# Two causal attentions with scores one head further ahead on the tensor engine, and four buffers that hold first scores, then probabilities

## The chip, the cores and the metric

The kernel runs on one core of a Trainium2 chip. The core has a tensor engine (PE in the profile, with its weight loads as PEld), a vector engine (DVE), a scalar engine (ACT), a general engine (POOL) and a queue that issues transfers (SP). Each engine runs its own list of instructions in order; they meet only at semaphores. The metric is the device time of one execution in microseconds, the median of three runs.

## The reference

The model has four blocks over 256 tokens of width 1024: an RWKV-7 time mix, a causal attention with 16 heads of width 64, an mLSTM with an MLP, and a latent attention (8 heads, values of width 128, keys of 128 plus 64 rotary) with another MLP. The two attentions compute the same thing per head:

```python
s = (jnp.einsum('bqhd,bkhd->bhqk', qn_b, k_nope)
     + jnp.einsum('bqhd,bkd->bhqk', qr_b, k_rope)).astype(jnp.float32) * scale
s = jnp.where(kpos[None, :] <= qpos[:, None], s, -jnp.inf)
p = jax.nn.softmax(s, axis=-1)
return jnp.einsum('bhqk,bkhd->bqhd', p.astype(v.dtype), v)
```

For the first attention the rotary term is inside `q` and `k`, and with 256 tokens its single block of 256 keys is the whole sequence. The scores of a head are thus a 256 x 256 lower triangle: 128 queries against 128 keys, and 128 queries against 256 keys, 384 columns in all.

## The kernel before

The whole program is one launch. Weights come from memory in 95 panels of 2 MB through a ring of four slots (`ring`); SP issues panel i once slot i - 4 has been used (L1221). Large products run as three products of rounded parts, so each panel is first split by ACT (high part, L1279 and L1292) and by DVE (low part, L1850 and L1863).

The function `attention` stands three times, once for each engine. It is called as "at1" (16 heads, L961) and as "at3" (8 heads, L1203). For each head h:

- PE, `score(h)`: the scores into one PSUM bank, "S". In at1 these are lines L958 and L959, in at3 L1197 to L1200.
- DVE: adds the causal mask, writes the masked scores to the buffer `Ss[h % 2]` in SBUF and takes the row maxima (L2239, twice, each with an accumulator read), then turns the maxima into biases (L2243).
- ACT: two exponentials from `Ss[h % 2]` into `Ps[h % 2]` with row sums (L1547, L1549).
- PE, `turn_p(h)`: three transposes of the probabilities into a bank "PT" (L614).
- ACT: copies them to `PTs[h % 2]` (the copy helper, L1336).
- PE, `pv(h)`: three products with the values into a bank "O" (L623, L625).
- DVE, `gather`: after every fourth head (at1) or second head (at3) the division by the row sums (L2226, L2229), and in at1 the gating (L2266).

The order on PE is written out: in step h it issues the scores of head h, the transposes of head h - 1, and the value products of head h - 2. Banks for S and PT come in turn from five banks. ACT's order is: exponentials of head h, copy of head h - 1, and in some steps a quarter of a weight panel's split (L1292: one quarter in each of the steps 1 to 8 of at1, two in each of the steps 1 to 4 of at3). DVE's order is: maxima of head h, a gather where one is due, in at3 a quarter of a row of the modulation table in odd steps (L1837), and quarters of the low parts (L1850: one in each of the steps 6 to 13 of at1, two in each of the steps 4 to 7 of at3).

Both buffers are two deep. DVE may write `Ss[h % 2]` once the exponentials of head h - 2 are done (L2236), and ACT may write `Ps[h % 2]` once the transposes of head h - 2 are done (L1545).

Of the kernel before, what the change touches and what calls it, by code (L numbers as in the profile page):

```python
# [10 lines left out]
ACT = mybir.ActivationFunctionType  # L11
# [90 lines left out]
def build(nc, x, cc_d, pc_d, pos_d, gn_d, sel_d, cond_d, stream, out, debug=None):  # L102

    order = []
    with ExitStack() as ctx:
# [5 lines left out]
        def sem(name):  # L111
            if name not in sems:
                sems[name] = ctx.enter_context(nc.semaphore(name))
            return sems[name]
# [60 lines left out]
        def finished(product):  # L175

            b, turn = place[product]
            return sem(f"bank_full{b}"), turn + 1
# [78 lines left out]
        def cols(n, a, b):  # L257
            return arena[:, n, a:b]

        Ss = cols(12, 0, 768).rearrange("p (a n) -> p a n", a=2)  # L260
        Ps = cols(12, 768, 1536).rearrange("p (a n) -> p a n", a=2)
        PTs = cols(14, 0, 768).rearrange("p (a n) -> p a n", a=2)


# [87 lines left out]
        def _(pe):  # L352
# [249 lines left out]
            def attention(name, heads, dv, scores, V):  # L602

                per = 512 // (TB * dv)

                def score(h):
                    b = claim((name, "S", h))
                    scores(h, b).then_inc(filled((name, "S", h)), 1)

                def turn_p(h):  # L610
                    b = claim((name, "PT", h))
                    pe.wait_ge(sem(name + "_p"), h + 1)
                    for n in range(3):
                        ins = nc.tensor.transpose(b[:, n * P:(n + 1) * P], Ps[:, h % 2, n * P:(n + 1) * P], ident)  # L614
                    ins.then_inc(filled((name, "PT", h)), 1)

                def pv(h):
                    if h % per == 0:
                        claim((name, "O", h // per), 5 + h // per % 2)
                    b = bank((name, "O", h // per))  # L620
                    pe.wait_ge(*evacuated((name, "PT", h)))
                    o = (h % per) * TB * dv
                    mm(b[:, o:o + dv], PTs[:, h % 2, 0:P], V[:, 0, h * dv:(h + 1) * dv], start=True, stop=True)  # L623
                    for kb in range(2):
                        ins = mm(b[:, o + dv:o + 2 * dv], PTs[:, h % 2, (1 + kb) * P:(2 + kb) * P],  # L625
                                 V[:, kb, h * dv:(h + 1) * dv], start=(kb == 0), stop=(kb == 1))
                    if h % per == per - 1:
                        ins.then_inc(filled((name, "O", h // per)), 1)
                    else:
                        ins.then_inc(pn.step(name + "_pv"), 1)  # L630


                kept, rotation["banks"] = rotation["banks"], list(range(5))
                for h in range(heads + 2):
                    if h < heads:
                        score(h)
                    if 1 <= h <= heads:
                        turn_p(h - 1)
                    if h >= 2:
                        pv(h - 2)  # L640
                rotation["banks"] = kept


# [616 lines left out]
        def _(act_):  # L1260
# [279 lines left out]
            def attention(name, heads, dv, scale, early):  # L1540
                for h in range(heads + 1):
                    if h < heads:

                        if h >= 2:
                            act_.wait_ge(*finished((name, "PT", h - 2)))  # L1545
                        act_.wait_ge(sem(name + "_max"), h + 1)
                        act(Ps[:, h % 2, 0:P], Ss[:, h % 2, 0:P], ACT.Exp, scale=scale, bias=nmax[:, h, 0:1],  # L1547
                                   accum_out=rs[:, h, 0:1]).then_inc(ac.step(), 1)
                        act(Ps[:, h % 2, P:3 * P], Ss[:, h % 2, P:3 * P], ACT.Exp, scale=scale, bias=nmax[:, h, 1:2],  # L1549
                                   accum_out=rs[:, h, 1:2]).then_inc(ac.step(name + "_p"), 1)  # L1550
                    if h >= 1:

                        if h >= 3:
                            act_.wait_ge(*pv_done(name, 512 // (TB * dv), h - 3))
                        copy(PTs[:, (h - 1) % 2, :], (name, "PT", h - 1), 3 * P)
                    for u, q in early.get(h, ()):
                        split_quarter(u, q)
# [200 lines left out]
        def _(dve):  # L1758
# [460 lines left out]
            def attention(name, heads, dvd, scale, O, early, between=None, gathered=None):  # L2219
                per = 512 // (TB * dvd)  # L2220

                def gather(g):
                    p = (name, "O", g)
                    dve.wait_ge(*finished(p))
                    hs = slice(g * per, (g + 1) * per)
                    V.reciprocal(rs[:, hs, :], rs[:, hs, :]).then_inc(dv.step(), 1)  # L2226
                    dve.wait_ge(*dv.last)
                    o = O[:, :, g * per * dvd:(g + 1) * per * dvd].rearrange("p b (h d) -> p h b d", d=dvd)
                    tt(o, bank(p)[:, :].rearrange("p (h b d) -> p h b d", h=per, b=TB),  # L2229
                                  rs[:, hs, :].unsqueeze(3).to_broadcast([P, per, TB, dvd]), ALU.mult).then_inc(dv.frees(p), 1)  # L2230

                done = 0
                for h in range(heads):

                    if h >= 2:
                        dve.wait_ge(sem(name + "_p"), h - 1)  # L2236
                    dve.wait_ge(*finished((name, "S", h)))
                    for tb, cs in ((0, slice(0, P)), (1, slice(P, 3 * P))):
                        V.tensor_tensor_reduce(Ss[:, h % 2, cs], bank((name, "S", h))[:, cs], con("causal")[:, cs], 1.0, 3.0 * NEG,  # L2239
                                               ALU.add, ALU.max, accum_out=mx[:, 2 * (h % 2) + tb:2 * (h % 2) + tb + 1]).then_inc(  # L2240
                            dv.frees((name, "S", h)) if tb else dv.step(), 1)
                    dve.wait_ge(*dv.last)
                    ts(nmax[:, h, :], mx[:, 2 * (h % 2):2 * (h % 2) + 2], -scale, None, ALU.mult).then_inc(dv.step(name + "_max"), 1)  # L2243
                    if (done + 1) * per <= h - 3:
                        gather(done)
                        done += 1
                    if between:
                        between(h)
                    for u, q in early.get(h, ()):
                        split_quarter(u, q)  # L2250
                while done * per < heads:
                    if gathered:
                        gathered(done)
                    gather(done)
                    done += 1
                if gathered:
                    gathered(done)
# [349 lines left out]
```

## Time and profile before

| | us |
|---|---|
| three runs | 1100.61, 1101.17, 1101.26 (median 1101.17) |
| the profiled execution | 1103.99 |
| its span, first to last instruction | 1102.2 |
| PE busy in the span | 1027.2 (93%) |
| DVE, ACT busy | 720.3 (65%), 511.0 (46%) |
| mean granted clock of PE | 0.977 of full speed |
| at1 runs from about | 387 to 422 |
| at3 runs from about | 851 to 874 |

A timeline row gives start, duration, engine, line, output and inputs, and in brackets how long the engine had been idle before it and what released it. Busy time of PE has modelled ends: rows that follow each other closely overlap. So the pace of PE is read from start to start, not from durations. A row "x3" merges three instructions in a row of the same line.

### The profile page before, as it was taken

To read this page: it belongs to the slowest core of one execution; us is meant where nothing else is said; L and a number is where in the kernel's file an instruction comes from. 1 tells how busy PE (TensorE), PEld (TensorE's weight loads), DVE (VectorE), ACT (ScalarE), POOL (GpSimd) and SP (SyncE) were. 2 spreads that over 40 slices of the span, in tenths; PEclk is the share of its full clock that TensorE was granted. 3 is DMA by queue.
4 is the path that set the end of the run, shared out by engine and by line. 5 is a ranking of instruction groups with operands and counts; after the bars stand their busy time and mean duration, and the time that the engine had idled before them with its cause. 6 is when DMAs were issued, how large, how long until landed. Compare 5 with 4: busy or idle time off the path is not lost.

```text
span 1102.2 us, 19472 instructions
## 1 busy us (share of the span) xinstructions
PE 1027.2 (93%) x8386; PEld 873.2 (79%) x8386; DVE 720.3 (65%) x1210; ACT 511.0 (46%) x780; POOL 33.2 (3%) x31
## 2 busy tenths in 40 slices
PE   5999999889998989999988999999889889999997
PEld 5784679887787867777766989998688759899995
DVE  6778248738889657655485785766588856644544
ACT  3424132135633585444354544555455746544542
POOL 0000025200000100000000000000000000000000
PEclk9999999999999999999988999999889999999998
DMA  9763301512476531556245577767725652665420
GB/s 382 301 247 126 153 1 32 224 61 78 153 303 231 187 119 51 190 219 229 77 153 229 199 288 297 285 238 303 298 78 208 250 197 110 215 243 208 175 78 38
DMA packets 15221, 205.39 MB, mean 186 GB/s; under 512 B 1816, under 2 KB 1816, under 8 KB 2976
## 3 DMA queue, kind: packets, MB, share of 16 engines
q1 hardware_dynamic: 14544, 202.55, 48.1%
q8 instruction: 66, 1.08, 0.4%
q10 hardware_dynamic: 592, 1.61, 0.4%
q14 instruction: 19, 0.16, 0.0%
HBM read 203.10 MB, written 1.05 MB: 185 GB/s over the span
## 4 chain that ended last, share of the span: by engine, by line
PE 78%; DVE 12%; DMA 4%; ACT 3%; issue 3%; SPq 0%; DVEq 0%; ACTq 0%
PE bank L452 16%; PE bank L453 16%; PE bank L454 16%; PE bank L746 5%; PE bank L545 5%; PE bank L401 4%; DMA ring<-in_stream 4%; DVE slot_parts L1863 2%; PE bank L558 2%; DVE ring L1837 2%; PE bank L652 1%; PE bank L730 1%; ACT page_parts L1279 1%; DVE arena L2324 1%; DVE arena L2239 1%
## 5 line engine op out<-in xcount | busy, mean ns | idle before, releaser
L452 PE MATMUL bank<-page_parts 128*128 128x512 f32 (+2 forms) x1190 | 406.5, 342 | 11.3 <-DVE slot_parts L1863 4.1
L1863 DVE TENSOR_TENSOR slot_parts<-ring,page_parts 128x2048 fp32r<-128x2048 f32 (+2 forms) x113 | 253.5, 2251 | 129.4 <-ACT page_parts L1279 128.8
L1279 ACT ACTIVATE page_parts<-ring 128x2048 fp32r<-128x2048 f32 (+2 forms) x113 | 211.5, 1883 | 138.1 <-PE bank L454 74.7
L452 PEld LDWEIGHTS bank<-page_parts 128*128 128x128 f32 x1190 | 228.1, 192 | 36.1 <-issue 10.6
L453 PE MATMUL bank<-slot_parts,page_parts 128*128 128x512 f32 (+2 forms) x622 | 243.5, 391 | 0.0
L454 PE MATMUL bank<-page_parts 128*128 128x512 f32 (+2 forms) x622 | 243.2, 391 | 0.0
L454 PE MATMUL bank<-page_parts,slot_parts 128*128 128x256 f32 x568 | 160.8, 283 | 0.0
L453 PE MATMUL bank<-page_parts 128*128 128x256 f32 x568 | 160.8, 283 | 0.0
L1336 ACT ACTIVATE arena<-bank 128x512 f32<-128x512 f32 (+2 forms) x134 | 73.8, 574 | 171.9 <-PE bank L454 57.4
L454 PEld LDWEIGHTS bank<-page_parts 128*128 128x128 f32 x622 | 118.9, 191 | 23.9
L453 PEld LDWEIGHTS bank<-slot_parts,page_parts 128*128 128x128 f32 x622 | 119.0, 191 | 22.5
L453 PEld LDWEIGHTS bank<-page_parts 128*128 128x128 f32 x568 | 109.0, 192 | 0.5
L454 PEld LDWEIGHTS bank<-page_parts,slot_parts 128*128 128x128 f32 x568 | 109.0, 192 | 0.0
L1837 DVE CUSTOM_DVE_ANT_0 ring<-ring,small 128x1024 f32<-128x1024 f32 x88 | 103.7, 1219 | 3.1 <-DMA ring<-in_stream 3.1
L558 PE MATMUL bank<-cc,arena 128*128 128x128 f32 x174 | 29.9, 340 | 33.8 <-DVE arena L1806 28.0
L746 PE MATMUL bank<-arena 64*64 64x64 f32 x1792 | 53.9, 218 | 6.4 <-issue 6.3
L746 PEld LDWEIGHTS bank<-arena 64*64 64x64 f32 x1792 | 53.1, 135 | 7.0 <-issue 7.0
L558 PEld LDWEIGHTS bank<-cc,arena 128*128 128x128 f32 x174 | 26.5, 179 | 39.4 <-DVE arena L1806 19.9
L545 PE MATMUL bank<-ring,arena 128*128 128x512 f32 x128 | 57.2, 607 | 0.0
L1614 ACT ACTIVATE arena<-bank 128x512 f32<-128x512 f32 x32 | 19.1, 596 | 69.9 <-PE bank L454 62.7
L545 PEld LDWEIGHTS bank<-ring,arena 128*128 128x128 f32 x128 | 24.8, 195 | 30.3 <-issue 30.3
L2078 DVE TENSOR_TENSOR arena<-arena,bank 128x512 f32<-128x512 f32 x36 | 23.9, 683 | 33.0 <-PE bank L746 32.7
(298 smaller groups left out, 1190.8 us busy)
## 6 DMA issues: line engine op xcount, KB each, us to landing
ring<-in_stream SPq DMA_DIRECT2D x95, 2048.0 KB, 8.3
arena<-in_x SPq DMA_DIRECT2D x2, 512.0 KB, 4.3
gn<-in_gn ACTq DMA_DIRECT2D x2, 512.0 KB, 17.3
out<-arena SPq DMA_DIRECT2D x2, 512.0 KB, 2.6
cc<-in_consts SPq DMA_DIRECT2D x1, 899.0 KB, 6.4
small<-in_cond ACTq DMA_DIRECT2D x1, 512.0 KB, 10.4
pc<-in_params SPq DMA_DIRECT2D x1, 287.5 KB, 6.7
gn<-in_head_sel ACTq DMA_DIRECT2D x1, 32.0 KB
```

What stands on the lines that cost most here:

```text
L401: ins = mm(b[:, half * T:(half + 1) * T], weights[:, k, ct * P:(ct + 1) * P], src[:, k, :], start=(k == 0), stop=(k == k_tiles - 1))
L452: mm(out, a[0], b[0], start=start, stop=False)
L453: mm(out, a[0], b[1], start=False, stop=False)
L454: return mm(out, a[1], b[0], start=False, stop=stop)
L545: ins = mm(b[:, 0:n], src[:, k, tb * P:(tb + 1) * P], weights[:, k, 0:n], start=(k == 0), stop=(k == k_tiles - 1))
L558: ins = nc.tensor.transpose(b[:, jj * T + tb * P:jj * T + (tb + 1) * P], src[:, tb, j * P:(j + 1) * P], ident)
L746: ins = mm(b[q * LC:(q + 1) * LC, j * LC:(j + 1) * LC], lhs(q, j), rhs(q, j), start=True, stop=True)
L1279: act(unit_parts(n)[0], unit_values(n)[1], ACT.Copy).then_inc(ac.step("w_hi"), 1)
L1336: act(dst, bank(product)[:, 0:n].rearrange("p (a b) -> p a b", a=dst.shape[1]) if len(dst.shape) == 3 else bank(product)[:, 0:n], kw.get(" ...
L1837: V.tensor_tensor_reduce(W, W, cond_row, 1.0, 0.0, ALU.mult, ALU.add, accum_out=ADA[:, at:at + 1]).then_inc(dv.step("ada_done" if ct == 3 ...
L1863: tt(unit_parts(n)[1], lo, hi, ALU.subtract).then_inc(dv.step("w_lo"), 1)
L2078: tt(dst[:, g], dst[:, g], bank((name, l, g))[:, :].rearrange("p (j t) -> p j t", j=8), ALU.subtract).then_inc(dv.frees((name, l, g)), 1)
```

## The change

The score and probability buffers become one array `Ps` of four buffers at the place of the former two and two. DVE writes the masked scores of head h to `Ps[h % 4]`, ACT takes the exponentials in place, and PE transposes from there. The wait of DVE before it writes becomes: the transposes of head h - 4 are done. The wait of ACT for the transposes of head h - 2 goes. On PE, step h now issues the scores of head h, the transposes of head h - 2 and the value products of head h - 3, in heads + 3 steps. `PTs` stays two deep, and everything else stays as it was.

```diff
-        Ss = cols(12, 0, 768).rearrange("p (a n) -> p a n", a=2)
-        Ps = cols(12, 768, 1536).rearrange("p (a n) -> p a n", a=2)
+        Ps = cols(12, 0, 1536).rearrange("p (a n) -> p a n", a=4)
...
-                        ins = nc.tensor.transpose(b[:, n * P:(n + 1) * P], Ps[:, h % 2, n * P:(n + 1) * P], ident)
+                        ins = nc.tensor.transpose(b[:, n * P:(n + 1) * P], Ps[:, h % 4, n * P:(n + 1) * P], ident)
...
-                for h in range(heads + 2):
+                for h in range(heads + 3):
                     if h < heads:
                         score(h)
-                    if 1 <= h <= heads:
-                        turn_p(h - 1)
-                    if h >= 2:
-                        pv(h - 2)
+                    if 2 <= h < heads + 2:
+                        turn_p(h - 2)
+                    if h >= 3:
+                        pv(h - 3)
...
-                        if h >= 2:
-                            act_.wait_ge(*finished((name, "PT", h - 2)))
                         act_.wait_ge(sem(name + "_max"), h + 1)
-                        act(Ps[:, h % 2, 0:P], Ss[:, h % 2, 0:P], ACT.Exp, scale=scale, bias=nmax[:, h, 0:1],
+                        act(Ps[:, h % 4, 0:P], Ps[:, h % 4, 0:P], ACT.Exp, scale=scale, bias=nmax[:, h, 0:1],
                                    accum_out=rs[:, h, 0:1]).then_inc(ac.step(), 1)
-                        act(Ps[:, h % 2, P:3 * P], Ss[:, h % 2, P:3 * P], ACT.Exp, scale=scale, bias=nmax[:, h, 1:2],
+                        act(Ps[:, h % 4, P:3 * P], Ps[:, h % 4, P:3 * P], ACT.Exp, scale=scale, bias=nmax[:, h, 1:2],
                                    accum_out=rs[:, h, 1:2]).then_inc(ac.step(name + "_p"), 1)
...
-                    if h >= 2:
-                        dve.wait_ge(sem(name + "_p"), h - 1)
+                    if h >= 4:
+                        dve.wait_ge(*finished((name, "PT", h - 4)))
                     dve.wait_ge(*finished((name, "S", h)))
                     for tb, cs in ((0, slice(0, P)), (1, slice(P, 3 * P))):
-                        V.tensor_tensor_reduce(Ss[:, h % 2, cs], bank((name, "S", h))[:, cs], con("causal")[:, cs], 1.0, 3.0 * NEG,
+                        V.tensor_tensor_reduce(Ps[:, h % 4, cs], bank((name, "S", h))[:, cs], con("causal")[:, cs], 1.0, 3.0 * NEG,
```

On PE at the start of at1, before the change (L958 and L959 are scores, L614 transposes, L623 and L625 value products; `at1_p` counts heads whose exponentials are done, `bank_free` a bank that has been read out):

```order
L958 MATMUL bank0<-arena 128x128 [waits bank_free0,zeros,bank_free5]
L959 MATMUL bank0<-arena 128x256
L958 MATMUL bank1<-arena 128x128 [waits bank_free1]
L959 MATMUL bank1<-arena 128x256
L614 MATMUL bank2<-cc,arena 128x128 [waits at1_p,bank_free2]
L614 MATMUL bank2<-cc,arena 128x128 x2
L958 MATMUL bank3<-arena 128x128 [waits bank_free3]
L959 MATMUL bank3<-arena 128x256
L614 MATMUL bank4<-cc,arena 128x128 [waits at1_p,bank_free4]
L614 MATMUL bank4<-cc,arena 128x128 x2
L623 MATMUL bank5<-arena 128x64 [waits bank_free2,bank_free5]
L625 MATMUL bank5<-arena 128x64 x2
```

And in the changed kernel at the same place (all its lines from there on have numbers lower by one):

```order
L957 MATMUL bank0<-arena 128x128 [waits bank_free0,zeros,bank_free5]
L958 MATMUL bank0<-arena 128x256
L957 MATMUL bank1<-arena 128x128 [waits bank_free1]
L958 MATMUL bank1<-arena 128x256
L957 MATMUL bank2<-arena 128x128 [waits bank_free2]
L958 MATMUL bank2<-arena 128x256
L613 MATMUL bank3<-cc,arena 128x128 [waits at1_p,bank_free3]
L613 MATMUL bank3<-cc,arena 128x128 x2
L957 MATMUL bank4<-arena 128x128 [waits bank_free4]
L958 MATMUL bank4<-arena 128x256
L613 MATMUL bank0<-cc,arena 128x128 [waits at1_p,bank_free0]
L613 MATMUL bank0<-cc,arena 128x128 x2
```

Three groups of scores now stand ahead of the first transposes instead of two, and so it stays through both attentions.

On DVE, the masked maxima of heads 3 and 4 of at1 before (the row with two waits is a head's first; the bias row has the wait for DVE's own last step):

```order
L2239 ISA arena,small<-bank0,cc 128x128 [waits bank_full0,at1_p]
L2239 ISA small 128x1
L2239 ISA arena,small<-bank0,cc 128x256
L2239 ISA small 128x1
L2243 TENSOR_SCALAR small<-small 128x2 [waits bank_free0]
L2239 ISA arena,small<-bank2,cc 128x128 [waits bank_full2,at1_p]
```

And the same heads in the changed kernel:

```order
L2235 ISA arena,small<-bank4,cc 128x128 [waits bank_full4]
L2235 ISA small 128x1
L2235 ISA arena,small<-bank4,cc 128x256
L2235 ISA small 128x1
L2239 TENSOR_SCALAR small<-small 128x2 [waits bank_free4]
L2235 ISA arena,small<-bank1,cc 128x128 [waits bank_full1,bank_full3]
```

The wait for the exponentials (`at1_p`) has gone; from head 4 on a wait for a bank of transposes (`bank_full3`) stands in its place.

## Rows read from the trace of the kernel before

**Rows 1.** The page: the span
```profile
span 1102.2 us, 19472 instructions
```

**Rows 2.** Busy time by stretch, then clock, DMA share and GB/s
```profile
387.00:420.00 33.00, 27.71 (x194) 22.31 (x193) 20.45 (x95) 26.81 (x89) 0.00 (x0) 1.00 0.22 84
400.00:410.00 10.00, 8.90 (x63) 7.05 (x63) 7.73 (x33) 8.26 (x28) 0.00 (x0) 1.00 0.00 1
560.00:570.00 10.00, 8.36 (x32) 7.72 (x33) 8.79 (x13) 3.99 (x10) 0.00 (x0) 0.53 0.39 167
851.00:872.00 21.00, 17.49 (x121) 15.04 (x120) 17.15 (x61) 15.04 (x48) 0.00 (x0) 1.00 0.68 287
```

**Rows 3.** Waits in at1, 386 to 426 us: total, times, longest
```profile
ACT arena L1547 <- DVE small L2243: 6.2, 10, 0.9
PE bank L614 <- ACT arena L1549: 5.3, 9, 1.8
```

**Rows 4.** Timeline of at1, its start: start, duration, engine, line
```profile
390.24 0.39 PE L958 MATMUL bank<-arena 128*128 128x128 f32 x2
390.52 0.47 ACT L1336 ACTIVATE arena<-bank 128x384 f32<-128x384 f32 x1
390.89 0.62 ACT L1292 ACTIVATE page_parts<-ring 128x512 fp32r<-128x512 f32 x1
390.89 0.49 PE L614 MATMUL bank<-cc,arena 128*128 128x128 f32 x3
```

**Rows 5.** Timeline of at1, heads 3 to 5
```profile
395.05 0.52 PE L614 MATMUL bank<-cc,arena 128*128 128x128 f32 x3
...
395.30 0.29 DVE L2239 CUSTOM_DVE_ANT_0 arena<-bank,cc 128x128 f32<-128x128 f32 x1 [1.59 <-PE bank L959]
...
396.05 0.44 PE L958 MATMUL bank<-arena 128*128 128x128 f32 x2
396.24 0.40 ACT L1547 ACTIVATE arena<-arena,small 128x128 f32<-128x128 f32 x1 [0.44 <-DVE small L2243]
396.32 0.60 PE L959 MATMUL bank<-arena 128*128 128x256 f32 x2
...
397.07 0.29 DVE L2239 CUSTOM_DVE_ANT_0 arena<-bank,cc 128x128 f32<-128x128 f32 x1 [0.93 <-PE bank L959]
...
397.37 0.52 PE L614 MATMUL bank<-cc,arena 128*128 128x128 f32 x3 [0.45 <-ACT arena L1549]
397.50 0.62 ACT L1292 ACTIVATE page_parts<-ring 128x512 fp32r<-128x512 f32 x1
...
398.02 0.39 ACT L1547 ACTIVATE arena<-arena,small 128x128 f32<-128x128 f32 x1
```

**Rows 6.** Timeline of at1, DVE: heads 7 and 8
```profile
401.22 0.29 DVE L2239 CUSTOM_DVE_ANT_0 arena<-bank,cc 128x128 f32<-128x128 f32 x1 [0.40 <-PE bank L959]
...
403.48 0.29 DVE L2239 CUSTOM_DVE_ANT_0 arena<-bank,cc 128x128 f32<-128x128 f32 x1
```

**Rows 7.** Timeline of at1: the last transposes, head 15
```profile
419.79 0.52 PE L614 MATMUL bank<-cc,arena 128*128 128x128 f32 x3 [0.79 <-ACT arena L1549]
```

**Rows 8.** Exponentials elsewhere: L1444 into another buffer, L1445 in place
```profile
L1444 ACT ACTIVATE arena<-arena x2: 1040/1040/1041, 87.0 to 90.0; 128x1024 f32<-128x1024 f32 x2
...
L1445 ACT ACTIVATE arena<-arena x2: 1040/1040/1041, 88.0 to 90.9; 128x1024 f32<-128x1024 f32 x2
```

**Rows 9.** Timeline of at3: DVE at heads 4 to 7, last transposes
```profile
861.71 0.29 DVE L2239 CUSTOM_DVE_ANT_0 arena<-bank,cc 128x128 f32<-128x128 f32 x1 [0.46 <-PE bank L1200]
...
864.08 0.29 DVE L2239 CUSTOM_DVE_ANT_0 arena<-bank,cc 128x128 f32<-128x128 f32 x1 [0.33 <-PE bank L1200]
...
868.00 0.28 DVE L2239 CUSTOM_DVE_ANT_0 arena<-bank,cc 128x128 f32<-128x128 f32 x1
...
869.95 0.28 DVE L2239 CUSTOM_DVE_ANT_0 arena<-bank,cc 128x128 f32<-128x128 f32 x1
...
872.01 0.52 PE L614 MATMUL bank<-cc,arena 128*128 128x128 f32 x3 [0.73 <-ACT arena L1549]
```

## The prediction, made before the changed kernel ran

> **What bounds the kernel now.** I read the busy times by stretch first, to see which engine is short of work in the two attentions; then the waits of these stretches, to see who keeps it waiting; then the timeline, row by row, to find the loop that sets the pace of one head and what would set it once the order is changed.
>
> The table by stretch shows at1 as a place where nobody is full: of 33 us PE is busy 27.7, ACT 26.8, DVE 20.5; in at3, of 21 us, PE 17.5 and DVE 17.2. The granted clock is 1.00 in both, so no price here is a clock price [rows 2]. The waits name a ring: PE's transposes wait for the exponentials (5.3 us in 9 waits), the exponentials wait for the maxima (6.2 us in 10) [rows 3]; the maxima wait for the scores, and the scores stand behind the transposes and value products in PE's own list. In at3 the table leaves PE idle for 21.00 - 17.49 = 3.5 us [rows 2].
>
> The timeline gives the ring its size. In at1 the transposes of head 1 start at 390.89 and those of head 15 at 419.79 [rows 4, 7]: 28.90 us for 14 heads, 2.06 each. What each engine needs by itself is less:
>
> - PE. From transposes through value products to the next scores 1.00 (395.05 to 396.05) [rows 5]; scores to the next transposes, with nothing waited for, 0.65 (390.24 to 390.89) [rows 4]. That is 1.65. The scores are sometimes a little slower behind value products: their second line starts 0.27 after the first (396.05 to 396.32) [rows 5] where it was 0.22 at the start, so I take 1.70.
> - ACT. With a quarter of a panel in its step, one head costs 1.78 from exponentials to exponentials (396.24 to 398.02) [rows 5]. The quarter is 0.52 of it (397.50 to 398.02), so 1.26 without.
> - DVE. Its dearest step, with maxima, gather and quarter, takes 2.26 (401.22 to 403.48, the second row without a wait) [rows 6], but only one in four holds a gather. From 400 to 410 DVE is busy 7.73 us [rows 2], in which 10 / 2.06 = 4.9 heads pass: 1.6 a head.
>
> So the pace of 2.06 is a latency, not work. Along the ring: scores' second line to maxima 0.75 (396.32 to 397.07), maxima to exponentials 0.94 (395.30 to 396.24), exponentials to transposes 1.13 (396.24 to 397.37) [rows 5]. That is 2.82 and must fit, with copy and value products, into two steps of PE.
>
> **The change, part by part.**
>
> *Instructions.* None is added or removed: the same number of products, maxima, exponentials and copies. Two waits go (ACT's for the transposes of two heads back, DVE's for the exponentials of two heads back) and one comes: DVE's for the transposes of head h - 4. Behind that wait stand DVE's maxima and all of its panel quarters. But PE issues the transposes of head h - 4 in step h - 2, and DVE waits in the same place for the scores of step h anyway, which PE does later in its one list. The new wait costs nothing. The banks are the same: five in turn, and each claim still asks for one read out long ago (the transposes of head h ask for the bank of the scores of head h - 1 or h, both evacuated before its exponentials). I take 0 for all of it.
>
> *Exponentials in place.* Two other exponentials show what that costs: 1040 ns into another buffer and 1040 ns in place, for the same shape [rows 8]. So 0; the bound on the other side is a rival below.
>
> *at1, the new order.* The scores run one step further ahead, so 2.82 gets three steps. Now the work sets the pace. The start: transposes of head 0 as before, since they wait for the first exponentials; the scores of head 2 go into PE's wait. ACT starts the copy of head 0 at 390.52 and its first quarter at 390.89 [rows 4]; the quarter takes 0.52, and since the maxima of head 2 are ready by then, exponentials of head 2 start at 391.41, its transposes 1.13 later at 392.54. From there to head 9 ACT is the longest, 1.78 a head against 1.70 on PE: 392.54 + 7 x 1.78 = 405.0. From head 9 ACT has no quarters, DVE is at 1.6, and PE sets the pace: transposes of head 13 at 405.0 + 4 x 1.70 = 411.8. The last scores (head 15) stand just ahead of these; their second line starts 0.43 earlier, at 411.4. Now the latency shows once: 411.4 + 2.82 = 414.2 for the transposes of head 15, while PE by itself would be there at 411.8 + 2 x 1.00 = 413.8. Before it was 419.79 [rows 7]. Gain 5.6, and I take 5.6.
>
> The tail is the same from there: copy, last value products, gather, gating, output product. The gating of the first three quarters on DVE starts after the last maxima and their gather, which move as much.
>
> Bounds for this term: the reported idle of PE in the stretch, 33.00 - 27.71 = 5.3, and the whole of its wait if each of 14 heads went at 1.65 behind the start: 28.90 - 14 x 1.65 = 5.8. If ACT's pace of 1.78 held to the end, the gain would be 28.90 - 14 x 1.78 = 4.0. I take 4.0 and 5.8 as ends.
>
> *at3.* Here the middle is at its work limit already: ACT has two quarters in each of the steps 1 to 4 (the 1.26 and two quarters of 0.52: 2.30) and PE has four products for its scores, so the steps of before are 2.37 long (861.71 to 864.08 on DVE) [rows 9]. The change gains nothing there. But scores move one slot forward, and DVE is late at the end: it finishes head 5 with a gather, a row quarter and two panel quarters only at 868.00, when the scores of head 6 have waited long; PE's transposes then wait. Now the maxima of head 5 start in the slot at which head 4 started before, 861.71 in place of 864.08. From there DVE is in one piece: 868.00 - 864.08 = 3.92 to head 6, 869.95 - 868.00 = 1.95 to head 7 [rows 9], so head 7 starts at 867.58 instead of 869.95, and its transposes at 869.64 instead of 872.01. Gain 2.4. ACT is free by then: its steps 5 and 6 hold no quarters and take 1.26. DVE's low-part quarters in step 4 come a slot earlier too, while the high part they need is finished in ACT's step 2 and doesn't move; it is two slots ahead now, one then, and a wait there would take from the 2.4. Bounds: nothing, if DVE's step 4 slips by what the slot gains, and 3.5, all of PE's idle time [rows 2].
>
> *What follows.* DMA is still at 400 to 410 (1 GB/s) [rows 2]: all four slots are full and the next issue waits for a release by work behind at1. In at3 the last issue of its time is released by a row quarter of DVE in step 7, which moves too. So the stream starts earlier by as much as the work, and both gains are passed on whole.
>
> The sum, against the profiled execution: 1103.99 (span 1102.2 [rows 1] and 1.8 around it) - 5.6 - 2.4 = 1096.0. The profiled execution is 2.8 above the median, so the median becomes 1101.17 - 8.0 = 1093.2.
>
> **A rule against it.** After at1 and at3 nothing changes but the hour. Yet after each long pause of PE its granted clock is half for a while, as at 560 to 570, mean 0.53 [rows 2], nearly all of it at 1.2 GHz and not at 2.4. This costs up to 10 x 0.47 = 4.7 us there. The Trainium skill ("TensorE: Matmul & The Clock Gate", Part 1: The HAM clock gate) says that the gate's observation runs on by itself and isn't set by the kernel's start, so that the same kernel sees its slow stretches differ from run to run. By that rule a shift of 8 us can't be cheap or dear in itself; it redraws the draws, and the sum stays. The three runs before lie within 0.65 us, so the draws are small here.
>
> **The rivals.**
>
> 1. *Only half arrives.* The at1 gain stops at ACT's pace (4.0) and at3 gives nothing since DVE's step 4 slips: 1097.2. For it: DVE is busy 17.2 of 21 in at3 [rows 2], and what the high part leaves at 861.7 is little. Against: DVE's chain behind it has no wait for anything that stays in place.
> 2. *The change doesn't do what it says.* The pace of at1 stays 2.06, because ACT's copy of head h - 1 now waits for transposes that PE issues a step later, and exponentials stand behind that copy. Per head ACT would then have to wait 0.28 (2.06 - 1.78), and the time is 1101. Against: the transposes of head h - 1 end 0.65 + 0.52 [rows 4, 5] into step h + 1, copy and quarter (0.37 and 0.52) and the exponentials' 1.13 follow, 3.2 in all with the semaphores left out, and the transposes of head h + 1 start only 2 x 1.78 + 0.65 = 4.2 after the same point: 1.0 to spare.
> 3. *Slower: the clock after the attentions.* Place: the pauses of PE between stages behind 424 us. Price: a further slow stretch like that of 560 to 570 costs 4.7 [rows 2]. It decides from two further ones on, or if existing ones get longer by 10.2 us in all: 8.0 given back and 2.2 lost, 1103.4. For it: such stretches exist behind every pause, and their length depends on when the pause falls. Against: the pauses keep their lengths and the spread of runs is 0.65.
> 4. *Slower by the exponentials in place.* Each of 24 heads would need some 0.45 more to eat the gain: half again of 0.89 (1.26 less the copy's 0.37 [rows 4]). The rows show no difference at all at 1024 columns [rows 8].
>
> **How the numbers follow.** My forecast (a gain of 6 to 10) has a chance of 0.75, rival 1 0.11, rival 2 0.06, rivals 3 and 4 together 0.06, and 0.02 is for a gain over 10. What a measurement of this kernel can tell from no change is about 0.2%, 2.2 us. Faster is the forecast, rival 1 and a larger gain: 0.88; same is rival 2: 0.06; slower 0.06. The range for 8 in 10 goes from 1090.7 (both upper ends, 5.8 + 3.5, and 1.2 for the draws of the clock) to 1098.2 (rival 1 and 1.0 for them).
>
> **What the changed profile would show.** Right: the transposes of at1 come at steps of 1.78 to head 9 and of about 1.70 behind it, with nearly no wait for exponentials; one wait is left at head 15; PE's idle in at1 falls from 5.3 to under 1.5; DVE in at3 runs from head 5 to the end without a wait, and the last transposes are 2.4 nearer to the first maxima. Wrong: a pace of at1 near 2.06, ACT's copies waiting for the transposes, exponentials longer than 0.40 and 0.49, or equal attentions with longer stretches at half clock behind them.

## The result, and the profile after

The changed kernel takes 1096.06 us (median of 7 runs, 1092.81 to 1098.66) against 1101.29 for the kernel before in the same comparison (7 runs, 1100.61 to 1105.49). The ratio over all of these runs is 0.9939, with a 95% interval of [0.9921, 0.9957]: faster by 0.4 to 0.8% (the two medians alone give 0.9953, the two means 0.9935). Forecast was 1093.2 within 1090.7 to 1098.2. One later run of the changed kernel, of 1172 us at a mean clock of 0.837, was disturbed and is left out of all medians and means below.

The profiled execution took 1092.81 us, 11.2 less than the one of before. That is more than the change gave; 3.1 of it lies ahead of the first attention, in code that is the same (first scores at 383.5 us, before at 386.6), and 2.5 between the attentions (from the last transposes of the first to the first maxima of the second 430.7 us, before 433.2). Further profiles show that both are spread, with no effect of the change to be seen: between the attentions the kernel before took 433.2, 430.0 and 431.1, the changed one 430.7, 429.9 and 433.3. So the stretches of the attentions are compared by themselves. The page and the busy times by stretch of the changed kernel:

```profile
span 1091.0 us, 19448 instructions
```

```profile
383.50:411.00 27.50, 26.13 (x195) 22.86 (x194) 19.95 (x95) 26.46 (x89) 0.00 (x0) 1.00 0.27 107
842.00:858.00 16.00, 14.87 (x106) 13.12 (x104) 14.56 (x55) 13.84 (x47) 0.00 (x0) 1.00 0.75 318
```

PE now idles 1.4 of 27.5 us in the first attention, where it idled 5.3 of 33 [rows 2]. (Its busy time fell too, from 27.7 to 26.1 us, with the same products in it: rows that stand closer together overlap more.) The waits of that stretch, 386 to 413 us:

```profile
DVE arena L2235 <- PE bank L958: 5.9, 9, 1.3
PE bank L613 <- ACT arena L1545: 1.4, 2, 1.1
ACT arena L1543 <- DVE small L2239: 0.5, 1, 0.5
```

Against [rows 3] the exponentials' wait for maxima fell from 6.2 us in 10 to 0.5 in one, the transposes' wait for exponentials from 5.3 in 9 to 1.4 in 2. The 1.1 is the wait of head 0 at the start, which was 1.8 before. The timeline of PE's transposes (L613 now; start, duration), heads 0 to 4, then 8 to 15:

```profile
386.77 0.52 PE L613 MATMUL bank<-cc,arena 128*128 128x128 f32 x3 [1.11 <-ACT arena L1545]
387.79 0.49 PE L613 MATMUL bank<-cc,arena 128*128 128x128 f32 x3
389.44 0.49 PE L613 MATMUL bank<-cc,arena 128*128 128x128 f32 x3
391.19 0.52 PE L613 MATMUL bank<-cc,arena 128*128 128x128 f32 x3
392.96 0.52 PE L613 MATMUL bank<-cc,arena 128*128 128x128 f32 x3
...
400.04 0.52 PE L613 MATMUL bank<-cc,arena 128*128 128x128 f32 x3
401.81 0.52 PE L613 MATMUL bank<-cc,arena 128*128 128x128 f32 x3
403.58 0.49 PE L613 MATMUL bank<-cc,arena 128*128 128x128 f32 x3
405.24 0.49 PE L613 MATMUL bank<-cc,arena 128*128 128x128 f32 x3
406.89 0.49 PE L613 MATMUL bank<-cc,arena 128*128 128x128 f32 x3
408.55 0.49 PE L613 MATMUL bank<-cc,arena 128*128 128x128 f32 x3
409.49 0.50 PE L613 MATMUL bank<-cc,arena 128*128 128x128 f32 x3
410.87 0.52 PE L613 MATMUL bank<-cc,arena 128*128 128x128 f32 x3 [0.26 <-ACT arena L1545]
```

Two paces can be read off: 1.77 while ACT has a panel quarter in each step (391.19 to 392.96) and 1.65 behind it (405.24 to 406.89). Only the last step waits for the latency. Heads 1 to 15 take 23.08 us; they took 28.90 [rows 4, 7]. What ACT does in one of the 1.77 steps:

```profile
391.84 0.39 ACT L1543 ACTIVATE arena<-arena,small 128x128 f32<-128x128 f32 x1
...
392.22 0.50 ACT L1545 ACTIVATE arena<-arena,small 128x256 f32<-128x256 f32 x1
...
392.71 0.47 ACT L1335 ACTIVATE arena<-bank 128x384 f32<-128x384 f32 x1
...
393.08 0.62 ACT L1291 ACTIVATE page_parts<-ring 128x512 fp32r<-128x512 f32 x1
...
393.60 0.39 ACT L1543 ACTIVATE arena<-arena,small 128x128 f32<-128x128 f32 x1
```

No row has an idle note: ACT is full in this step. In the second attention DVE's maxima of heads 6 and 7 and the transposes behind them:

```profile
854.21 0.28 DVE L2235 CUSTOM_DVE_ANT_0 arena<-bank,cc 128x128 f32<-128x128 f32 x1
...
856.16 0.28 DVE L2235 CUSTOM_DVE_ANT_0 arena<-bank,cc 128x128 f32<-128x128 f32 x1
...
856.21 0.52 PE L613 MATMUL bank<-cc,arena 128*128 128x128 f32 x3 [0.41 <-ACT arena L1545]
...
858.17 0.52 PE L613 MATMUL bank<-cc,arena 128*128 128x128 f32 x3 [0.74 <-ACT arena L1545]
```

From the maxima of head 6 to those of head 7 it is 1.95 as before [rows 9]; DVE is still the chain at the end, only entered earlier. DVE's first maxima are at 841.59, so the last transposes stand 16.6 behind them; before it was 852.99 to 872.01, 19.0.

### The profile page after: what moved, and what is told of

Same layout as the page of the kernel before. It is cut to its first block, busy times and chain, and to the rows that moved or that the text cites. A ratio compares the mean times of both kernels' runs of the same rounds, so it can differ in the third digit from the quotient of the medians.

```text
span 1091.0 us, 19448 instructions
## 1 busy us (share of the span) xinstructions
PE 1023.4 (94%) x8386; PEld 873.3 (80%) x8386; DVE 720.0 (66%) x1210; ACT 510.9 (47%) x780; POOL 32.9 (3%) x31
## 4 chain that ended last, share of the span: by engine, by line
PE 79%; DVE 12%; DMA 3%; ACT 3%; issue 2%; SPq 0%; DVEq 0%; ACTq 0%
PE bank L451 16%; PE bank L452 16%; PE bank L453 16%; PE bank L745 5%; PE bank L544 5%; PE bank L400 4%; DMA ring<-in_stream 3%; DVE slot_parts L1859 3%; PE bank L557 2%; PE bank L651 1%; PE bank L729 1%; ACT page_parts L1278 1%; DVE arena L2320 1%; DVE ring L1833 1%; PE bank L624 1%
## 5 line engine op out<-in xcount | busy, mean ns | idle before, releaser
L451 PE MATMUL bank<-page_parts 128*128 128x512 f32 (+2 forms) x1190 | 405.3, 341 | 11.2 <-DVE slot_parts L1859 4.1
L451 PEld LDWEIGHTS bank<-page_parts 128*128 128x128 f32 x1190 | 227.3, 191 | 36.6 <-issue 10.6
L557 PE MATMUL bank<-cc,arena 128*128 128x128 f32 x174 | 30.2, 342 | 33.7 <-DVE arena L1802 27.7
L1610 ACT ACTIVATE arena<-bank 128x512 f32<-128x512 f32 x32 | 19.1, 597 | 73.7 <-PE bank L453 64.0
L2333 DVE TENSOR_TENSOR page_parts<-arena,page_parts 128x512 fp32r<-128x512 f32 x32 | 22.1, 689 | 35.4 <-ACT page_parts L1614 35.4
## 6 DMA issues: line engine op xcount, KB each, us to landing
gn<-in_gn ACTq DMA_DIRECT2D x2, 512.0 KB, 16.5
```

What stands on the lines that cost most here:

```text
L451: mm(out, a[0], b[0], start=start, stop=False)
L557: ins = nc.tensor.transpose(b[:, jj * T + tb * P:jj * T + (tb + 1) * P], src[:, tb, j * P:(j + 1) * P], ident)
L2333: tt(AF_LO[:, n % 2, 2 * i:2 * i + 2, :], a, hi, ALU.subtract).then_inc(dv.step("relu2"), 1)
```

## The experiments

All were timed or profiled beside the kernel before. The table takes from each profile the stretch from the transposes of head 1 to those of head 15 (at1), from DVE's first maxima to the last transposes in at3, and from there to the end.

| kernel | at1 | at3 | behind at3 | median, runs | ratio to before |
|---|---|---|---|---|---|
| before, three profiles | 28.9, 28.9, 28.9 | 19.0, 19.3, 19.1 | 230.2, 230.1, 230.2 | 1102.9 (23) and 1103.6 (11) | |
| changed, three profiles | 23.1, 23.1, 23.1 | 16.6, 16.5, 16.8 | 232.8, 232.9, 232.8 | 1095.9 (6) and 1097.1 (5) | 0.9933 [0.9913, 0.9953]; 0.9936 [0.9916, 0.9957] |
| order only | 23.15 | 16.8 | 232.3 | 1095.8 (6) | 0.9939 [0.992, 0.9958] |
| buffers only | 28.4 | 19.1 | 232.8 | 1105.0 (12) | 1.0015 [0.9997, 1.0033] |
| order in at3 only | 28.4 | 16.8 | 232.8 | 1102.3 (12) | 0.9991 [0.9974, 1.0008] |
| quarters spread | 23.5 | 16.9 | 232.8 | 1095.2 (1) | |
| row quarters later | 23.1 | 15.7 | 236.2 | 1097.1 (1) | |
| three heads ahead, two profiles | 22.5, 22.5 | 16.5, 16.7 | 229.9, 232.8 | 1094.3 (1) and 1097.1 (6) | 0.9937 [0.9921, 0.9953] |
| three ahead and quarters spread | 21.8 | 16.6 | 232.9 | 1095.0 (6) | 0.9919 [0.9903, 0.9935] |

Beside the single timings the kernel before took 1102.9. The ratios of the two kernels with three heads ahead, and the second median and ratio of the first two rows, come from one comparison, the other ratios from an earlier one.

**The changed kernel again.** Nothing is edited.

> The changed kernel once more, beside the kernel before on one chip, to size the gain against the spread. Theory 1 (the attentions gain 5.8 and 2.5 us, as the two traces show from the first transposes of head 1 to the last, and nothing is given back behind them): the median is 8.3 us under the kernel before, give or take 1.5, at equal mean clock. Theory 2 (part of it is given back behind the attentions in stretches of PE at half clock): 4 to 6 us under, with a lower mean granted clock than before. Whatever the median, transposes of head 1 to head 15 in the first attention take 23.1 us, as they did, and not 28.9.

The stretch is 23.1 again (23.09, and 23.08 the first time). The median is 6.9 below the kernel before in its comparison, at the lower end of theory 1 and above what theory 2 said, but with a lower clock than before (0.977 against 0.978 on average), which theory 1 had set equal; more on it below.

**The order alone.** In the kernel before:

```diff
-                for h in range(heads + 2):
+                for h in range(heads + 3):
...
-                    if 1 <= h <= heads:
-                        turn_p(h - 1)
-                    if h >= 2:
-                        pv(h - 2)
+                    if 2 <= h < heads + 2:
+                        turn_p(h - 2)
+                    if h >= 3:
+                        pv(h - 3)
```

> Only the new order on PE (scores of head h, transposes of head h - 2, value products of head h - 3); the buffers stay two and two as before, with both old waits. Theory 1 (the pace was set by the order on PE alone; two buffers each are enough, since the exponentials of head h start about 2.9 us after the transposes of head h - 2 that free their buffer): the same gain as the whole change, 23.1 us from the transposes of head 1 to head 15 and 8 us in all. Rival (the buffers limit how far the scores run ahead; without four in turn the new order waits for them): 26 us or more, and less than half of the gain.

23.15 and 16.8, and a ratio of 0.9939: the gain is there without the four buffers, up to 0.07 us of the first attention. The rival falls. The old buffers show once: the maxima of head 2 wait 0.7 us for the exponentials of head 0 (390.36, released by ACT's L1549), and the transposes do not feel it, since head 1 to head 9 take 14.02 us in both kernels.

**The buffers alone.** In the changed kernel:

```diff
-                for h in range(heads + 3):
+                ahead = 1
+                for h in range(heads + ahead + 1):
...
-                    if 2 <= h < heads + 2:
-                        turn_p(h - 2)
-                    if h >= 3:
-                        pv(h - 3)
+                    if ahead <= h < heads + ahead:
+                        turn_p(h - ahead)
+                    if h >= ahead + 1:
+                        pv(h - ahead - 1)
```

> Only the four buffers and the exponentials in place; PE keeps the order of before. Theory 1: 0 us, 28.9 us from the transposes of head 1 to head 15, exponentials at 0.40 and 0.49 as before. Rival (the two waits that went were part of the ring): the stretch is under 27 us. Second rival (in place costs): exponentials over 0.45 and 0.54, slower by 1 us or more.

28.4 instead of 28.9: a gain of half a microsecond where theory 1 said none, and far from the rival. The second rival has its answer in the exponentials' rows (min/median/max in ns), in this kernel and then in the kernel before:

```profile
L1544 ACT ACTIVATE arena<-arena,small x24: 385/401/403, 390.2 to 868.5; 128x128 f32<-128x128 f32 x24
...
L1546 ACT ACTIVATE arena<-arena,small x24: 491/492/498, 390.6 to 868.9; 128x256 f32<-128x256 f32 x24
```

```profile
L1547 ACT ACTIVATE arena<-arena,small x24: 385/402/403, 388.7 to 870.9; 128x128 f32<-128x128 f32 x24
...
L1549 ACT ACTIVATE arena<-arena,small x24: 491/492/496, 389.1 to 871.3; 128x256 f32<-128x256 f32 x24
```

401 and 492 ns in place, 402 and 492 before. Its median is 2.1 us higher, but the ratio of 1.0015 has 1 inside its interval, and at equal granted clock (the line is told below) it lies 0.1 above the kernel before, give or take 0.8; its attentions are not longer.

Where the half microsecond comes from can be read in the rows: bias and first exponential of head 4, before (the exponential is in [rows 5], 396.24) and with "buffers only":

```profile
395.97 0.17 DVE L2243 TENSOR_SCALAR small<-small 128x2 f32<-128x2 f32 x1
```

```profile
397.29 0.17 DVE L2240 TENSOR_SCALAR small<-small 128x2 f32<-128x2 f32 x1
...
397.49 0.40 ACT L1544 ACTIVATE arena<-arena,small 128x128 f32<-128x128 f32 x1 [0.38 <-DVE small L2240]
```

Before, the exponential had two waits and started 0.26 behind the bias; now it has one and starts 0.20 behind it. The same 0.06 stands at every head from head 2 on, although the wait that went, for transposes of two heads back, had long been met. The maxima of heads 2 and 3, which have no second wait in this kernel, start 0.64 behind the scores' second line and not 0.74; from head 4 on, with the new second wait, it is 0.74 again. One such delay lies in every second step of the loop: 0.16 is gained up to head 2, 0.48 up to head 14, 0.52 up to head 15. That it is the wait is shown for DVE within one kernel; for ACT it is argued, since the buffer changed in the same edit. The 1.1 us that DVE waits before for ACT's L1549 ahead of head 15 cost nothing: here the same row waits 1.06 for the scores.

**The order in the second attention alone.** The same edit with `ahead = 2 if name == "at3" else 1`.

> The changed kernel with the order of before on PE in the first attention, so that only the second (8 heads) has the new order; the buffers are four in both. Theory 1: the first attention takes 28.9 us from head 1 to head 15, the second has its last transposes 16.7 us after DVE's first maxima as in the changed kernel and not 19.0 as before, and the time is 2.4 us under the kernel before. Rival (the 2.5 of the second attention is not passed on, since the panels behind it come no earlier): the same 16.7, and a time equal to before.

The second attention came out as said (16.8); the first took 28.4 and not 28.9, as with "buffers only". The time did not settle it: a ratio of 0.9991 [0.9974, 1.0008] allows a gain of up to 2.9 us, and so 2.4 as well as none. At equal granted clock it lies 2.1 below the kernel before, give or take 0.8, which fits passing it on; and so does the table: behind at3 this kernel and "buffers only", which differ in the order in at3 alone, have the same 232.8.

**A second and a third profile of before.** Nothing is edited.

> The kernel before once more, for a second profile. Theory 1 (the change gives nothing back behind the attentions; the differences there between the two first profiles are draws of PE's clock): 28.9 us again from the transposes of head 1 to head 15, and from the last transposes of the second attention to the end about 232.9 us, as in the changed kernel and in the three variants, not 230.2 as in the first profile. Theory 2 (the stage behind the attentions is longer with the change): 230.2 us again.

> The kernel before a third time, for one more profile. Theory 1 (the half-clock stretch behind the second attention comes in a short and a long form by a draw that has nothing to do with the attentions): 230.2 or 232.9 us from the last transposes of the second attention to the end; with 232.9 the long form is shown in the kernel before too, with 230.2 it stays open whether it is rarer there. Theory 2 (it belongs to the changed kernel alone): 230.2.

230.1 and 230.2. So the 232.9 that theory 1 gave for the second profile was wrong, and the third leaves its second form open, as said beforehand. More on it under the clock behind the second attention.

**ACT's quarters spread.**

```diff
-            attention("at1", NH, HD, 0.125, {n + 1: [(u + n // 4, n % 4)] for n in range(8)})
+            attention("at1", NH, HD, 0.125, {(1, 2, 4, 5, 7, 8, 10, 11)[n]: [(u + n // 4, n % 4)] for n in range(8)})
```

and DVE's quarters in the steps 6 to 9, 12, 13 and two in 14.

> The changed kernel with ACT's eight panel quarters of the first attention in the steps 1, 2, 4, 5, 7, 8, 10, 11 in place of 1 to 8, and DVE's in 6 to 9 and 12 to 14. Theory 1 (with the new order ACT's 1.77 a head is the bound as long as each step holds a quarter, and PE's 1.65 behind it): transposes of head 1 to head 9 take 13.3 to 13.6 us and not 14.0, and head 1 to head 15 22.5 us, not 23.1. Rival (PE's list with its semaphores can't go faster than 1.75 beside busy engines): 23.1 again.

Half right. Where a step had no quarter, PE went at 1.66 at once; head 1 to head 9 took 13.8, not 14.0, nor the 13.3 to 13.6 I said. But the stretch as a whole grew to 23.5. Its timeline at the end:

```profile
406.87 0.69 DVE L1846 TENSOR_TENSOR slot_parts<-ring,page_parts 128x512 fp32r<-128x512 f32 x1 [0.88 <-ACT page_parts L1291]
...
409.57 1.29 DVE L1846 TENSOR_TENSOR slot_parts<-ring,page_parts 128x512 fp32r<-128x512 f32 x2
...
410.78 0.28 DVE L2235 CUSTOM_DVE_ANT_0 arena<-bank,cc 128x128 f32<-128x128 f32 x1
...
412.78 0.52 PE L613 MATMUL bank<-cc,arena 128*128 128x128 f32 x3 [0.78 <-ACT arena L1545]
```

DVE runs ahead of ACT and so waited 0.88 for the later quarter, and its double quarter pushed the last maxima out: the transposes of head 15 wait 0.78, where they waited 0.26. The bound had moved to the engine that was given the work. The rival (no pace under 1.75) falls by the 1.66.

**Row quarters later.**

```diff
-            attention("at3", MH, DV, MLA_SCALE, O3, quarters_from(4, u, 2), lambda h: ada(h % 2))
+            attention("at3", MH, DV, MLA_SCALE, O3, quarters_from(4, u, 2), lambda h: ada(h % 2 if h < 4 else 0))
             split_output("wo_d", "o3T", O3_PAGES)
+            ada(2)
```

> The changed kernel with DVE's two row quarters of the steps 5 and 7 of the second attention moved behind the splits of the output product. Theory 1 (the second attention's end is DVE's chain of work): the last transposes stand 1.1 us nearer to the first maxima, 15.4 and not 16.5 us. Rival (ACT or PE take over as the bound at once): 16.2 or more. The panel that the last row quarter releases is issued later by some 15 us; if that is felt, the stage behind grows from 232.9 by up to the 1.1 or more.

15.7: 0.8 to 1.1 nearer than in the three profiles of the changed kernel, so DVE's work is the chain there. But the stage behind grew by 3.4, more than was expected. The release of the ring slot came so late that ACT waited for the next panel:

```profile
885.05 3.71 ACT L1278 ACTIVATE page_parts<-ring 128x2048 fp32r<-128x2048 f32 x2 [8.25 <-DMA ring<-in_stream]
```

In the changed kernel no such wait stands at this place, and PE's pause ahead of the next products, 5.1 us there, is 8.4 here.

**Three heads ahead.** `ahead = 3` in both attentions, still four buffers.

> The changed kernel with scores yet another head ahead (in step h scores of head h, transposes of head h - 3, value products of head h - 4), still four buffers. Theory 1 (the latency no longer sets the pace, the work of ACT and PE does): the pace in the middle stays, 1.77 and then 1.65; at most 1 us less from the first scores to the last transposes of the first attention (27.4 before), from work put into the wait before the first transposes; the second stays at 16.5 within 0.3, since DVE is full there. Rival (latency still counts): 2 us or more less.

> Scores three heads ahead once more, timed beside the changed kernel. Theory 1: 26.7 us from the first scores to the last transposes of the first attention as in its first profile, 0.6 less than the changed kernel, and a median 0.6 under the changed kernel's: less than these runs can tell from nothing. Rival (the shift also moves the half-clock stretch behind the second attention out of its long form, which its one profile didn't have): a median 3 us under the changed kernel's.

From first scores to last transposes of at1 26.7 both times, where the changed kernel has 27.3: a fourth group of scores fits into the first wait (1.11 down to 0.46), the last wait of 0.26 is gone, and the middle keeps its paces. The median is that of the changed kernel beside it (1097.1 both), so the rival falls; its second profile has the long form behind at3 (232.8).

**Both together.** `ahead = 3`, ACT's quarters in the steps 1, 2, 3, 5, 6, 7, 9, 10, DVE's in 7 to 10, 12, 13 and two in 14.

> The same with ACT's quarters in the steps 1, 2, 3, 5, 6, 7, 9, 10 and DVE's in 7 to 10 and 12 to 14 of the first attention. Theory 1 (ACT's quarters set the pace to head 9, and DVE's stacked quarters were what spoiled the first attempt): 26.1 us from the first scores to the last transposes. Rival (DVE's two quarters in step 14 delay the last maxima again): 26.7 or more.

26.1 as said. Its transposes go at 1.65 from head 5 to head 12; heads 5 to 7:

```profile
398.88 0.49 PE L613 MATMUL bank<-cc,arena 128*128 128x128 f32 x3
400.54 0.49 PE L613 MATMUL bank<-cc,arena 128*128 128x128 f32 x3
402.19 0.49 PE L613 MATMUL bank<-cc,arena 128*128 128x128 f32 x3
```

With one more head of lead the late quarters on DVE no longer hold the last transposes up. It has the largest gain of its comparison, 0.9919 [0.9903, 0.9935], the changed kernel beside it 0.9936 [0.9916, 0.9957]; but the intervals overlap. That the stretch is 1.25 us shorter is shown by its trace; that the whole kernel is, these times do not show.

**The changed kernel a third time.**

> The changed kernel a third time, for the comparison with the two above and for the clock. Theory 1: 23.1 us from the transposes of head 1 to head 15, a median 7 us under the kernel before; the stage behind the second attention 232.9 or 230.2 us by the draw of the clock. Theory 2 (the long form belongs to the changed kernel): 232.9.

23.1 and 232.8, which both theories allowed. The median is 6.5 under the kernel before, where 7 was said.

## Why the prediction was right, and where it was not

**The ring.** Right. 2.06 a head was latency: with one head more of lead and no other edit ("order only") it went to 1.77 and 1.65. The latency still shows once, in the wait of head 15 (0.26): from the scores' second line at 408.11 to the transposes at 410.87 it is 2.76, the 2.82 of the forecast less the 0.06 of ACT's dropped wait.

**The paces.** ACT's 1.78 measured 1.77; PE's 1.70 measured 1.65, the lower of the two readings I had. Heads 1 to 9 took 14.0 (forecast 14.1), heads 1 to 15 23.1 (forecast 23.3). The term of at1: 5.6 forecast, 5.8 measured, which is at the upper end that I gave. The other bound there, PE's reported idle of 5.3, was none: the gain is larger, since PE's busy time shrank as well.

**In place, and the waits.** In place 0, by the rows of "buffers only". The waits I had set to 0 by asking only whether they are met in time. They are; DVE never waits for the transposes of four heads back. But a second wait on an instruction costs by being there: with ACT's dropped the exponentials start 0.06 earlier, and with the old order that, and the 0.10 of DVE's once, added up to 0.5. With the new order only the last step feels it: 23.15 for "order only", 23.08 with the whole change.

**What the change is said to need.** I took order and buffers as one. The runs part them: by the stretches the order does all but 0.07 us. The totals are less sharp: at equal clock "order only" lies 7.4 below before, give or take 1.0, the changed kernel 8.4, give or take 0.7.

**at3.** 2.4 forecast, 2.2 to 2.8 measured between profiles. The mechanism is as forecast: the maxima of head 5 stand 8.70 us behind the first ones (850.29 after 841.59), where head 4 stood before (861.71 after 852.99, 8.72), and DVE's chain behind it kept its 3.92 and 1.95.

**The sum.** 8.0 forecast. By stretches the gain is 5.8 + 2.5 = 8.3. By medians it was 5.2, then 6.9 and 6.5; over the two later comparisons of before and all three of the changed kernel, the mean of before is 1103.0 (34 runs) and that of the changed kernel 1096.0 (18 runs): 7.0. The step that failed in size is "so the draws are small here", which I had drawn from three runs within 0.65 us. More runs of the kernel before went from 1099.65 to 1106.12. Each run has its mean granted clock, and it explains most of the spread: a straight line through 94 runs of seven kernels, each kernel with its own level, has 0.64 us for each 0.001 of clock. Before averaged 0.9785, the changed kernel 0.9763. At equal clock the levels differ by 8.4, give or take 0.7 (95%), which is the stretches' gain. So some 1.4 us of it were taken by the clock, of the sort of rival 3, but far from its price of 10.2. The forecast of 1093.2 lies 2.9 too low mostly for two reasons outside the attentions: the median that I started from, 1101.2, was 1.8 under the mean of the 34 runs, and the clock took the 1.4.

**The clock behind the second attention.** There it can be seen. Rows by 2 us, some 35 us behind the last transposes: the changed kernel (893 to 905), then the kernel before (906.9 to 914.9); the third number from the end is the clock:

```profile
893.00:895.00 2.00, 0.23 (x1) 0.23 (x2) 1.65 (x4) 0.00 (x0) 0.00 (x0) 0.71 0.98 418
895.00:897.00 2.00, 2.00 (x11) 2.00 (x11) 0.00 (x0) 1.01 (x3) 0.00 (x0) 0.50 1.02 438
897.00:899.00 2.00, 2.00 (x12) 2.00 (x10) 1.89 (x4) 2.00 (x6) 0.00 (x0) 0.50 0.36 143
899.00:901.00 2.00, 2.00 (x10) 2.00 (x11) 1.93 (x5) 2.00 (x3) 0.00 (x0) 0.50 0.00 0
901.00:903.00 2.00, 2.00 (x12) 2.00 (x11) 2.00 (x2) 0.61 (x2) 0.00 (x0) 0.50 0.00 0
903.00:905.00 2.00, 2.00 (x14) 2.00 (x14) 2.00 (x2) 0.00 (x0) 0.00 (x0) 0.73 0.00 0
```

```profile
906.90:908.90 2.00, 0.29 (x2) 0.30 (x3) 1.58 (x4) 0.00 (x0) 0.00 (x0) 0.98 0.96 410
908.90:910.90 2.00, 2.00 (x12) 2.00 (x11) 0.18 (x1) 1.23 (x3) 0.00 (x0) 0.50 1.06 446
910.90:912.90 2.00, 2.00 (x15) 2.00 (x13) 1.93 (x5) 2.00 (x6) 0.00 (x0) 0.67 0.27 115
912.90:914.90 2.00, 2.00 (x19) 2.00 (x19) 1.93 (x5) 2.00 (x3) 0.00 (x0) 1.00 0.00 0
```

PE has paused 5.1 us for the norm ahead of both. From the clock column the half clock (1.2 instead of 2.4 GHz) runs from about 893.9 to 904.1 in the changed kernel, three times as long as from 908.8 to 912.2 in the kernel before. That goes with the 2.6 us between 232.8 and 230.2: the same work stands in both. Of eleven profiles of the other kernels, the changed one among them, ten have the long form (232.3 to 236.2, the last with its late panel), "three heads ahead" once the short one and once the long one; "buffers only" has the long one with the order of before. So it belongs neither to a shorter attention nor to one program alone. In all fourteen profiles the form goes with the place of the start: in the ten long ones the half clock starts 34.6 to 35.8 us behind the last transposes, in the four short ones 36.0 to 36.8, while PE takes up work again at 36.6 (row quarters later: 39.9). That the kernel before had the late start three times out of three stays unexplained; the runs can't tell whether its odds are better. So a part of the 1.4 us may belong to the change after all. The Trainium skill ("TensorE: Matmul & The Clock Gate", Part 1: The HAM clock gate) says the gate's observation runs on by itself; by that rule one program differs from run to run, and the trace agrees: 229.9 and 232.8 from one kernel.

## What to carry to other kernels

When every engine in a loop has idle time and the waits form a ring, add up the latency around the ring and compare it with the lead that the written order gives: one more step of lead costs no instruction and gives back the difference, up to the pace of the busiest engine. Test order and buffers apart: the buffers may not be what limits. Count the waits on the ring too, met or not. And read a gain of under one per cent from the stretch it was made in, with the granted clock beside the total, since one stretch of half clock elsewhere moved the total here by 2.6 us, a third of the gain.

## What the runs showed of the hardware

- A stretch of half clock behind a pause of some 5 us of PE has two lengths for the same work, about 3.4 and 10.2 us, and 2.6 us of time between them (230.2 and 232.8 behind the second attention). The long one starts 0.8 to 2.0 us ahead of PE's first product behind the pause, the short one from 0.6 us ahead of it to 0.2 behind it.
- Exponentials in place in SBUF take what they take into another buffer: 401 and 492 ns against 402 and 492 ns for 128 and 256 columns.
- A second semaphore wait that has long been met delays the start all the same: the masked maxima on DVE start 0.74 and not 0.64 us behind the scores' second line (heads 4 on against heads 2 and 3 of "buffers only"). An exponential on ACT starts 0.26 behind its bias row before and 0.20 with "buffers only", where its buffer changed too.
- Code ahead of the change took 383.5 to 389.6 us over the 14 profiles, though it is the same in all; the mean granted clock up to there was 1.00 in the first and 0.98 in the last.
